# Two transformer blocks on one core: another order of loads, modulation pieces and first norm

## The chip, the cores and the metric

The kernel runs on one core of a Trainium2 chip. The metric is the time on the device of one execution, in microseconds (us). An instruction or a row is located by its line in the kernel file (L2190 is line 2190). The engines are PE (TensorE, matrix products; PEld are its weight loads), DVE (VectorE), ACT (ScalarE), POOL (GpSimd) and SP (SyncE), which here only issues DMAs. Each engine executes its own list of instructions in order, and waits on semaphores for the others.

## The reference

All in float32, for 512 tokens of width 1024, with 256 context tokens. The part that matters here is the first lines of the first block:

```python
sh1, sc1, gt1, sh2, sc2, gt2 = split(silu(c) @ w_mod + b_mod, 6)        # for the tokens
csh1, csc1, ...              = split(silu(c_ctx) @ w_mod + b_mod, 6)    # for the context
pc = (rmsnorm(ctx, norm1_g) * (1 + csc1) + csh1) @ w_in
px = (rmsnorm(x, norm1_g) * (1 + sc1) + sh1) @ w_in
```

`rmsnorm` divides each token by the root of the mean of its squares. From `pc` and `px` come a gated linear attention in both directions and a differential attention; their outputs go through `w_out`, then follow a gated feed-forward layer and a second block (pooling and forgetting attention, attention to a memory of 256 tokens, a convolved feed-forward layer). The scalar `lam` of the differential attention is made of the exponentials of two sums of products (lambda).

## The kernel before

Everything is held transposed: features on the 128 partitions, tokens along the free dimension; `xT` is 8 tiles (k = 0 to 7) of 128 x 512, `cmT` 8 of 128 x 256. A product of float32 quality is made of three passes in the type fp32r: high part of the weights by high part of the data, high by low, and low by high. For each unit of weights (128 x 1024, 512 KB) SP loads `raw` (4 buffers), ACT writes the high part `whi` (`hi`, L560 to 565, 3 buffers), and DVE, or POOL for units 1 and 2, the low part `wlo` (`lo`, L1239 to 1246, and L2008 to 2011). Units 0 to 3 are those of the first projection (`gqk`), two values of k each; unit 4 is that of the next product (`gd`).

There is no planner; the order is written out by hand for each engine, and this is the order at the start.

- SP (from L517): 16 pieces of the modulation weights (`mod1`, 512 KB each, two values of k by 512 columns), the context behind the sixth, the tokens behind the ninth, weight unit 0 behind the thirteenth, then units 1 to 3 and eight constants. Pieces 14 and 15 wait until PE has finished pieces 0 and 1 (`mdp`).
- PE (from L2157): eight transposes turn the condition (both vectors) into columns; ACT puts SiLU on them. The 16 pieces are multiplied in order, each by two columns, in plain float32 (L2190; four matmul records per piece), to rows of 512 results in banks 0, 1, 6 and 7, four pieces each. Ahead of piece 10 stand `turn_mods(0)` (eight small transposes that turn the first half of the rows to columns, L2166), the sum of the context's squares over the partitions (a product with ones, L2173), and the small lambda product in bank 3 (L2182); ahead of piece 11 the sum of the tokens' squares. Behind piece 15 come two products that broadcast the raw condition to all partitions (L2195, banks 0 and 1), and then the first projection (L2232 to 2242): for each k four banks (0 to 3) of 128 x 512 for the tokens, then two (4 and 5) of 128 x 256 for the context, each of three passes. `turn_mods(1)` follows k = 1. `fill(b)` waits for whoever last read bank b; `unit(j)` waits for `lo` of unit j.
- ACT (from L592): the squares of the context's and the tokens' tiles (L613), with the copies `mod_rows(0)` of the first two result rows (L602) between them; the roots (`root`: Ln, Exp, Square); the exponential of the lambda sums (L617, it frees bank 3); then a loop over i = 0 to 15, tile k = i // 2 of the tokens (i even) or of the context (i odd): it writes the high part of the normed tile (L630). At i = 4 stand `mod_rows(1)` and SiLU of the broadcast condition (L624, `cbx`), which frees banks 0 and 1; after i = 1, 3 and 7 `hi` of unit 0, 1 and 2.
- DVE (from L1271): adds the squares (L1277), finishes the roots (`newton`, L1255 and 1257), and in a loop over the same i, at i = 0 and 8, `first_mods` (L1287 and 1290: gains and shifts from the turned rows), `first_norm(i)` (L1300: tile x gain x root), `first_rest(i - 1)` (L1307: low part), and `lo(0)` at i = 2. Units 3 and up are split behind the loop.
- From there on `cbx` serves DVE for dot products that make the other modulations (L1328).

The products of k need their tile's low part (`x_ready`, `xc_ready`).

Of the kernel before, what the change touches and what calls it, by code (L numbers as in the profile page):

```python
# [16 lines left out]
D = 1024  # L17
# [168 lines left out]
def build(nc, ap, out):  # L186
# [6 lines left out]
    with ctx:  # L193
# [314 lines left out]
        def _(e):  # L508
# [8 lines left out]
            for n in range(16):  # L517
                w.wait_ge(s.mdp, n - 13)
                j = NU + n
                src = ap["weights"][offs[j]:offs[j + 1]].rearrange("(p k c) -> p k c", p=128, c=512)  # L520
                e.dma_start(mod1[n][:, :, :], src).then_inc(s_m[n % 14], 16)
                if n == 5:
                    e.dma_start(cmT[:, :, :], ap["ctx"]).then_inc(s.cm, 16)
                if n == 8:
                    e.dma_start(xT[:, :, :], ap["x"]).then_inc(s.x, 16)
                if n == 12:
                    load(0)
            for j in range(1, 4):
                load(j)
# [19 lines left out]
        def _(e):  # L549
# [48 lines left out]
            def mod_rows(half):  # L598
                for j in range(2):
                    w.wait_ge(s.mdp, 8 * half + 4 * j + 4)  # L600
                    b = 6 + j if half else j
                    e.activation(mrow[half][0:2, j, :], bank(b)[0:2, :], ACT.Copy).then_inc(s.mdr, 1)  # L602

            for q in range(16):
                if q == 8:
                    mod_rows(0)
                n, src, first = (256, cmT, acc_c) if q < 8 else (512, xT, acc)
                if q % 8 == 0:
                    w.wait_ge(*((s.cm, 16) if q == 0 else (s.x, 16)))
                elif q >= 4:  # L610
                    w.wait_ge(s.sqs, adds(q - 4))
                dst = tmp[q % 4] if q % 8 else first
                e.activation(dst[:, 0:n], src[:, q % 8, :], ACT.Square).then_inc(s.sq, 1)  # L613
            w.wait_ge(s.g_const, 1)
            root("ctx", bank(4, 256), 256, D)
            w.wait_ge(s.lam_p, 1)
            e.activation(small[:, 4:6], bank(3, 2), ACT.Exp).then_inc(s.lam_a, 1)  # L617
            root("x", bank(5), 512, D)
            for i in range(16):
                if i == 4:  # L620
                    mod_rows(1)
                    for j in range(2):
                        w.wait_ge(s.p_cb, 2 + j)
                        e.activation(cbx[:, 512 * j:512 * j + 512], bank(j), ACT.Silu).then_inc(s.cb, 1)  # L624
                        table[0] = "silu"
                k, ctx_ = i // 2, i % 2
                n = 256 if ctx_ else 512
                dst = (hch if ctx_ else hxh)[:, k, :]
                w.wait_ge(s.mt, nt_at["A", i])
                e.activation(dst, tmp[i % 4][:, 0:n], ACT.Identity, bias=modv[:, k, ctx_:ctx_ + 1]).then_inc(s.mh, 1)  # L630
                if i in (1, 3, 7):
                    hi(i // 3)
# [601 lines left out]
        def _(e):  # L1234
# [43 lines left out]
            newton("ctx", bank(4, 256), 256, D)  # L1278
            newton("x", bank(5), 512, D)

# [22 lines left out]
            def first_rest(i):  # L1303
# [4 lines left out]
                                       f((hch if c else hxh)[:, k, :]), ALU.add, ALU.subtract).then_inc(s.ml, 1)  # L1308

            for i in range(16):  # L1310
                if i % 8 == 0:
                    first_mods(i // 2)
                first_norm(i)
                if i:
                    first_rest(i - 1)
                if i == 2:
                    lo(0)
            first_rest(15)
# [770 lines left out]
        def _(e):  # L2089
# [80 lines left out]
            def first_sums(b, size, value, sum_):  # L2170
                w.wait_ge(s.sqs, value)
                w.wait_ge(s.g_const, 2)
                e.matmul(bank(b, size), ones[:, :], sum_[:, 0:size], start=True, stop=True).then_inc(s.p_sum, 1)  # L2173

            w.wait_ge(s.cb, 1)
            for n in range(16):
                if n == 10:
                    turn_mods(0)
                    first_sums(4, 256, 7, acc_c)
                    w.wait_ge(s.lam_v, 1)  # L2180
                    fill(3)
                    e.matmul(bank(3, 2), ones[:, :], small[:, 2:4], start=True, stop=True).then_inc(s.lam_p, 1)  # L2182
                    freed[3] = [(s.lam_a, 1)]
                if n == 11:
                    first_sums(5, 512, 14, acc)
                b = (0, 1, 6, 7)[n // 4]
                w.wait_ge(s_m[n % 14], 16 * (n // 14 + 1))
                for kk in range(2):
                    k = 2 * (n % 4) + kk
                    mm = e.matmul(bank(b)[0:2, :], cols_c[:, k, :], mod1[n][:, kk, :], start=(k == 0), stop=(k == 7))  # L2190
                mm.then_inc(s.mdp, 1)
            for j in range(2):
                w.wait_ge(s.mdr, j + 1)
                w.wait_ge(s.g_const, 2)
                e.matmul(bank(j), ones[0:1, :], crow[0:1, 512 * j:512 * j + 512], start=True, stop=True).then_inc(s.p_cb, 1)  # L2195
                freed[j] = [(s.cb, 2 + j)]
            freed[2] = [(s.mdv, 2)]
# [27 lines left out]
            for k in range(8):  # L2225
# [17 lines left out]
                if k % 2:  # L2243
                    mm.then_inc(s.used, 1)
                if k == 1:
                    turn_mods(1)
                    freed[6] = [(s.mdv, 4)]
                    freed[7] = [(s.mdr, 4)]
# [684 lines left out]
```

## Time and profile before

| what | value |
|---|---|
| median of 3 runs | 1654.87 us (1654.38 to 1655.11) |
| the profiled execution: its time | 1654.45 us |
| the profiled execution: its span | 1652.8 us |
| PE busy | 1578.4 us (96%) |
| DVE, ACT, POOL busy | 57%, 44%, 8% |
| DMA queue of SP | 152 MB |

The span runs from the first to the last instruction; its own time has 1.65 us more. A busy PE isn't a PE at its peak, since matmuls overlap and their ends are modelled. The page cuts the span into 40 slices of 41.3 us. In a timeline a row has the start and the length in us, engine, line, operation, what is written and read, the shapes and the number of merged instructions, and in brackets how long the engine had been idle and who released it.

### The profile page before, as it was taken

The numbers are of one execution on the slowest core, as the hardware profiler recorded it, in microseconds if no ns is written. First come the engines' busy times: TensorE is split into PE (matmuls) and PEld (weight loads), VectorE is DVE, ScalarE is ACT, GpSimd is POOL, SyncE is SP. The second block draws the span as 40 slices with busy tenths as digits, with TensorE's granted clock in tenths as the row PEclk, the third lists the DMA queues.
The fourth block names the chain that finished last, engine by engine and source line by source line (L and its number), as shares of the span: only waits on it lengthen the run. The fifth ranks groups of instructions, "written<-read, shape, count | busy, mean of one in ns | idle before, by whom it ended". The sixth has DMA issues, their size and how long they took to land.

```text
span 1652.8 us, 19178 instructions
## 1 busy us (share of the span) xinstructions
PE 1578.4 (96%) x7606; PEld 1241.7 (75%) x7606; DVE 938.5 (57%) x1441; ACT 732.8 (44%) x1132; POOL 124.2 (8%) x89
## 2 busy tenths in 40 slices
PE   8999999889899999999999899999977999999999
PEld 2777876677688888888878677788665788888885
DVE  3676777884834433334645555366556686257743
ACT  4444445675433222223443767455455443234432
POOL 0100213530000000000000111130010000000000
PEclk9999999699999999999999999999988999999999
DMA  9441111102433233222232222143202232333221
GB/s 375 156 166 52 52 52 59 56 1 88 155 132 136 75 106 113 99 78 92 90 102 70 75 67 65 63 129 103 77 27 89 65 115 70 109 115 97 79 91 53
DMA packets 47950, 156.60 MB, mean 95 GB/s; under 512 B 5587, under 2 KB 10323, under 8 KB 47350
## 3 DMA queue, kind: packets, MB, share of 16 engines
q1 hardware_dynamic: 47280, 152.00, 27.8%
q10 hardware_dynamic: 582, 3.38, 0.6%
q8 instruction: 61, 1.00, 0.2%
q14 instruction: 27, 0.22, 0.0%
HBM read 153.26 MB, written 2.10 MB: 94 GB/s over the span
## 4 chain that ended last, share of the span: by engine, by line
PE 79%; DVE 11%; ACT 6%; issue 3%; DMA 0%; POOL 0%; ACTq 0%; DVEq 0%
PE pall L2112 19%; PE pall L2113 18%; PE pall L2114 18%; PE pall L2596 2%; PE pall L2130 1%; PE pall L2132 1%; PE pall L2131 1%; PE pall L2148 1%; PE pall L2598 1%; PE pall L2597 1%; PE pall L2150 1%; PE pall L2149 1%; DVE wlo L1244 1%; DVE statd L1589 1%; PE pall L2190 1%
## 5 line engine op out<-in xcount | busy, mean ns | idle before, releaser
L1244 DVE TENSOR_TENSOR wlo<-raw,whi 128x1024 fp32r<-128x1024 f32 (+2 forms) x261 | 290.5, 1114 | 315.3 <-ACT whi L564 315.2
L564 ACT ACTIVATE whi<-raw 128x1024 fp32r<-128x1024 f32 (+2 forms) x263 | 247.0, 941 | 212.6 <-PE pall L2114 177.3
L2112 PE MATMUL pall<-h5h,whi 128*128 128x512 f32 x320 | 125.7, 393 | 2.5 <-DVE wlo L1244 2.5
L2113 PE MATMUL pall<-h5l,whi 128*128 128x512 f32 x320 | 125.2, 391 | 0.0
L2114 PE MATMUL pall<-h5h,wlo 128*128 128x512 f32 x320 | 125.0, 391 | 0.0
L2112 PE MATMUL pall<-h2h,whi 128*128 128x512 f32 x320 | 124.5, 389 | 0.0
L2113 PE MATMUL pall<-h2l,whi 128*128 128x512 f32 x320 | 124.5, 389 | 0.0
L2114 PE MATMUL pall<-h2h,wlo 128*128 128x512 f32 x320 | 124.5, 389 | 0.0
L2112 PEld LDWEIGHTS pall<-h5h,whi 128*128 128x128 f32 x320 | 60.4, 189 | 15.6 <-issue 3.1
L2114 PEld LDWEIGHTS pall<-h5h,wlo 128*128 128x128 f32 x320 | 60.5, 189 | 12.7
L2113 PEld LDWEIGHTS pall<-h5l,whi 128*128 128x128 f32 x320 | 60.5, 189 | 12.7 <-issue 0.2
L2114 PEld LDWEIGHTS pall<-h2h,wlo 128*128 128x128 f32 x320 | 60.1, 188 | 12.6
L2113 PEld LDWEIGHTS pall<-h2l,whi 128*128 128x128 f32 x320 | 60.1, 188 | 12.4
L2112 PEld LDWEIGHTS pall<-h2h,whi 128*128 128x128 f32 x320 | 60.1, 188 | 12.4
L2112 PE MATMUL pall<-fh,whi 128*128 128x512 f32 x176 | 68.5, 389 | 0.0
L2113 PE MATMUL pall<-fl,whi 128*128 128x512 f32 x176 | 68.5, 389 | 0.0
L2114 PE MATMUL pall<-fh,wlo 128*128 128x512 f32 x176 | 68.5, 389 | 0.0
L2112 PE MATMUL pall<-ch,whi 128*128 128x512 f32 x176 | 68.5, 389 | 0.0
L2113 PE MATMUL pall<-cl,whi 128*128 128x512 f32 x176 | 68.5, 389 | 0.0
L2114 PE MATMUL pall<-ch,wlo 128*128 128x512 f32 x176 | 68.5, 389 | 0.0
L946 ACT ACTIVATE fh<-tmp 128x512 fp32r<-128x512 f32 x22 | 13.9, 632 | 95.1 <-DVE tmp L1695 95.1
L1912 DVE TENSOR_TENSOR pall<-pall,R 128x512 f32<-128x512 f32 x48 | 33.1, 694 | 35.2 <-PE pall L2114 31.2
(460 smaller groups left out, 3644.8 us busy)
## 6 DMA issues: line engine op xcount, KB each, us to landing
raw<-in_weights SPq DMA_DIRECT2D x204, 512.0 KB, 3.5
mraw<-in_wmod SPq DMA_DIRECT2D x32, 512.0 KB, 5.1
mod<-in_weights SPq DMA_DIRECT2D x16, 512.0 KB, 12.2
raw<-in_weights SPq DMA_DIRECT2D x25, 256.0 KB, 2.5
raw<-in_weights SPq DMA_DIRECT2D x32, 192.0 KB, 2.3
xT<-in_x SPq DMA_DIRECT2D x1, 2048.0 KB, 17.0
xT<-in_x ACTq DMA_DIRECT2D x1, 2048.0 KB, 8.2
out_y<-xT SPq DMA_DIRECT2D x8, 256.0 KB, 2.1
```

Of the source, the lines that this page charges most:

```text
L564: e.activation(whi[j % 3][:, 0:cols(j)], raw[j % 4][:, 0:cols(j)], ACT.Copy).then_inc(s.hi, 1)
L1244: e.tensor_tensor(wlo[j % 3][:, 0:n], raw[j % 4][:, 0:n], f(whi[j % 3][:, 0:n]), ALU.subtract).then_inc(s.lo_v, 1)
L1589: e.reduce_max(sd[:, col:col + 1], bank(2 * dpair[c, n], 768), AX.X).then_inc(s.mx, 1)
L1912: e.tensor_tensor(bank(b), bank(b), r, ALU.mult).then_inc(s.rq, 1)
L2112: e.matmul(o_, a[:, kk, :], xh(k), start=(k == 0), stop=False)
L2113: e.matmul(o_, a[:, kk, :], xl(k), start=False, stop=False)
L2114: mm = e.matmul(o_, b[:, kk, :], xh(k), start=False, stop=(k == nk - 1))
L2130: e.matmul(bank(o_), a[:, k % 2, c], xh(k), start=(k == 0), stop=False)
L2131: e.matmul(bank(o_), a[:, k % 2, c], xl(k), start=False, stop=False)
L2132: mm = e.matmul(bank(o_), b[:, k % 2, c], xh(k), start=False, stop=(k == 7))
L2148: e.matmul(bank(o_), h_, a[:, kk, :], start=(k + kk == 0), stop=False)
L2596: e.matmul(bank(b), a[:, k, :], xh[:, k, :], start=(k == 0), stop=False)
```

## The change

SP issues the context and the tokens behind the fourth piece, weight unit 0 behind the eighth and unit 1 behind the twelfth. PE broadcasts the condition first (banks 6 and 7), does pieces 0 to 8 with the context's sum behind piece 5, turns the first half, sums the tokens' squares, and does pieces 9 to 11 and the lambda product; pieces 12 to 15 stand inside the projection behind k = 1, and `turn_mods(1)` behind k = 2. ACT does `cbx` first, then all squares, the context's root, `mod_rows(0)`, `hi(0)`, and the tokens' root; lambda's exponential stands at i = 6 of the loop, `mod_rows(1)` at i = 8. DVE does `first_mods(0)` and `lo(0)` before the tokens' root, and `first_rest(7)` before `first_mods(4)`.

```diff
--- before.py
+++ after.py
@@ -519,13 +519,12 @@
                 j = NU + n
                 src = ap["weights"][offs[j]:offs[j + 1]].rearrange("(p k c) -> p k c", p=128, c=512)
                 e.dma_start(mod1[n][:, :, :], src).then_inc(s_m[n % 14], 16)
-                if n == 5:
+                if n == 3:
                     e.dma_start(cmT[:, :, :], ap["ctx"]).then_inc(s.cm, 16)
-                if n == 8:
                     e.dma_start(xT[:, :, :], ap["x"]).then_inc(s.x, 16)
-                if n == 12:
-                    load(0)
-            for j in range(1, 4):
+                if n in (7, 11):
+                    load(n // 4 - 1)
+            for j in range(2, 4):
                 load(j)
             for dst, name in consts:
                 e.dma_start(dst, ap[name]).then_inc(s.const, 16)
@@ -601,9 +600,10 @@
                     b = 6 + j if half else j
                     e.activation(mrow[half][0:2, j, :], bank(b)[0:2, :], ACT.Copy).then_inc(s.mdr, 1)
 
+            for j in range(2):
+                w.wait_ge(s.p_cb, 2 + j)
+                e.activation(cbx[:, 512 * j:512 * j + 512], bank(6 + j), ACT.Silu).then_inc(s.cb, 1)
             for q in range(16):
-                if q == 8:
-                    mod_rows(0)
                 n, src, first = (256, cmT, acc_c) if q < 8 else (512, xT, acc)
                 if q % 8 == 0:
                     w.wait_ge(*((s.cm, 16) if q == 0 else (s.x, 16)))
@@ -613,22 +613,21 @@
                 e.activation(dst[:, 0:n], src[:, q % 8, :], ACT.Square).then_inc(s.sq, 1)
             w.wait_ge(s.g_const, 1)
             root("ctx", bank(4, 256), 256, D)
-            w.wait_ge(s.lam_p, 1)
-            e.activation(small[:, 4:6], bank(3, 2), ACT.Exp).then_inc(s.lam_a, 1)
+            mod_rows(0)
+            hi(0)
             root("x", bank(5), 512, D)
             for i in range(16):
-                if i == 4:
+                if i == 6:
+                    w.wait_ge(s.lam_p, 1)
+                    e.activation(small[:, 4:6], bank(3, 2), ACT.Exp).then_inc(s.lam_a, 1)
+                if i == 8:
                     mod_rows(1)
-                    for j in range(2):
-                        w.wait_ge(s.p_cb, 2 + j)
-                        e.activation(cbx[:, 512 * j:512 * j + 512], bank(j), ACT.Silu).then_inc(s.cb, 1)
-                        table[0] = "silu"
                 k, ctx_ = i // 2, i % 2
                 n = 256 if ctx_ else 512
                 dst = (hch if ctx_ else hxh)[:, k, :]
                 w.wait_ge(s.mt, nt_at["A", i])
                 e.activation(dst, tmp[i % 4][:, 0:n], ACT.Identity, bias=modv[:, k, ctx_:ctx_ + 1]).then_inc(s.mh, 1)
-                if i in (1, 3, 7):
+                if i in (3, 7):
                     hi(i // 3)
 
 
@@ -1276,7 +1275,6 @@
                     w.wait_ge(s.sqs, adds(q) - 1)
                     e.tensor_tensor(sum_[:, 0:n], sum_[:, 0:n], tmp[q % 4][:, 0:n], ALU.add).then_inc(s.sqs, 1)
             newton("ctx", bank(4, 256), 256, D)
-            newton("x", bank(5), 512, D)
 
             def first_mods(k):
 
@@ -1307,14 +1305,16 @@
                 e.scalar_tensor_tensor((hcl if c else hxl)[:, k, :], tmp[i % 4][:, 0:n], modv[:, k, c:c + 1],
                                        f((hch if c else hxh)[:, k, :]), ALU.add, ALU.subtract).then_inc(s.ml, 1)
 
+            first_mods(0)
+            lo(0)
+            newton("x", bank(5), 512, D)
             for i in range(16):
-                if i % 8 == 0:
-                    first_mods(i // 2)
+                if i == 8:
+                    first_rest(7)
+                    first_mods(4)
                 first_norm(i)
-                if i:
+                if i and i != 8:
                     first_rest(i - 1)
-                if i == 2:
-                    lo(0)
             first_rest(15)
             lo(2)
             w.wait_ge(s.cb, 3)
@@ -2172,28 +2172,34 @@
                 w.wait_ge(s.g_const, 2)
                 e.matmul(bank(b, size), ones[:, :], sum_[:, 0:size], start=True, stop=True).then_inc(s.p_sum, 1)
 
+            w.wait_ge(s.g_const, 2)
+            for j in range(2):
+                e.matmul(bank(6 + j), ones[0:1, :], crow[0:1, 512 * j:512 * j + 512], start=True, stop=True).then_inc(s.p_cb, 1)
+                freed[6 + j] = [(s.cb, 2 + j)]
             w.wait_ge(s.cb, 1)
-            for n in range(16):
-                if n == 10:
-                    turn_mods(0)
-                    first_sums(4, 256, 7, acc_c)
-                    w.wait_ge(s.lam_v, 1)
-                    fill(3)
-                    e.matmul(bank(3, 2), ones[:, :], small[:, 2:4], start=True, stop=True).then_inc(s.lam_p, 1)
-                    freed[3] = [(s.lam_a, 1)]
-                if n == 11:
-                    first_sums(5, 512, 14, acc)
+
+            def mod_piece(n):
                 b = (0, 1, 6, 7)[n // 4]
+                if n % 4 == 0:
+                    fill(b)
                 w.wait_ge(s_m[n % 14], 16 * (n // 14 + 1))
                 for kk in range(2):
                     k = 2 * (n % 4) + kk
                     mm = e.matmul(bank(b)[0:2, :], cols_c[:, k, :], mod1[n][:, kk, :], start=(k == 0), stop=(k == 7))
                 mm.then_inc(s.mdp, 1)
-            for j in range(2):
-                w.wait_ge(s.mdr, j + 1)
-                w.wait_ge(s.g_const, 2)
-                e.matmul(bank(j), ones[0:1, :], crow[0:1, 512 * j:512 * j + 512], start=True, stop=True).then_inc(s.p_cb, 1)
-                freed[j] = [(s.cb, 2 + j)]
+
+            for n in range(9):
+                mod_piece(n)
+                if n == 5:
+                    first_sums(4, 256, 7, acc_c)
+            turn_mods(0)
+            first_sums(5, 512, 14, acc)
+            for n in range(9, 12):
+                mod_piece(n)
+            w.wait_ge(s.lam_v, 1)
+            fill(3)
+            e.matmul(bank(3, 2), ones[:, :], small[:, 2:4], start=True, stop=True).then_inc(s.lam_p, 1)
+            freed[3] = [(s.lam_a, 1)]
             freed[2] = [(s.mdv, 2)]
             freed[4] = [(s.rsum, job["ctx"])]
             freed[5] = [(s.rsum, job["x"])]
@@ -2243,6 +2249,9 @@
                 if k % 2:
                     mm.then_inc(s.used, 1)
                 if k == 1:
+                    for n in range(12, 16):
+                        mod_piece(n)
+                if k == 2:
                     turn_mods(1)
                     freed[6] = [(s.mdv, 4)]
                     freed[7] = [(s.mdr, 4)]
```

## Rows read from the trace of the kernel before

**Rows 1.** The page, 40 slices of the span: granted clock of PE, and GB/s

```profile
PEclk9999999699999999999999999999988999999999
...
GB/s 375 156 166 52 52 52 59 56 1 88 155 132 136 75 106 113 99 78 92 90 102 70 75 67 65 63 129 103 77 27 89 65 115 70 109 115 97 79 91 53
```

**Rows 2.** Timeline of all engines, 0 to 110 us: the start

```profile
6.08 1.01 PE L2159 MATMUL pall<-ident,crow 2*128 2x2 f32 x8 [6.08 <-DMA ident<-in_ident]
...
7.37 19.61 PE L2190 MATMUL pall<-mod,small 128*2 128x512 f32 x40 [0.27 <-ACT small L596]
...
10.74 0.13 PEld L2190 LDWEIGHTS pall<-mod,small 128*2 128x2 f32 x1 [0.73 <-issue]
...
11.59 0.13 PEld L2190 LDWEIGHTS pall<-mod,small 128*2 128x2 f32 x1 [0.73 <-issue]
12.23 0.09 PEld L2190 LDWEIGHTS pall<-mod,small 128*2 128x2 f32 x1 [0.51 <-issue]
12.66 0.09 PEld L2190 LDWEIGHTS pall<-mod,small 128*2 128x2 f32 x1 [0.34 <-issue]
...
14.00 0.42 ACT L613 ACTIVATE acc_c<-cmT 128x256 f32<-128x256 f32 x1 [6.68 <-DMA cmT<-in_ctx]
```

**Rows 3.** The same timeline: the sums and the norm

```profile
27.50 0.70 PE L2173 MATMUL pall<-acc_c,ones 128*128 128x256 f32 x2
...
30.76 1.13 PE L2173 MATMUL pall<-acc,ones 128*128 128x512 f32 x2 [0.64 <-DVE acc L1277]
...
35.83 0.75 DVE L1300 SCALAR_TENSOR_TENSOR tmp<-xT,gsv,R 128x512 f32<-128x512 f32 x1
...
37.38 0.75 DVE L1307 SCALAR_TENSOR_TENSOR hxl<-tmp,modv,hxh 128x512 fp32r<-128x512 f32 x1 [0.40 <-ACT hxh L630]
```

**Rows 4.** The same timeline: the broadcasts and the start of the projection

```profile
40.49 1.98 PE L2195 MATMUL pall<-crow,ones 1*128 1x512 f32 x4
...
45.21 0.77 PE L2232 MATMUL pall<-hxh,whi 128*128 128x512 f32 x1 [2.74 <-ACT cbx L624]
```

**Rows 5.** Timelines of PE (50 to 78 us), then DVE, then ACT (45 to 135 us)

```profile
54.33 0.65 PE L2166 MATMUL pall<-ident,mrow 2*128 2x2 f32 x8
...
58.48 0.40 PE L2232 MATMUL pall<-hxh,whi 128*128 128x512 f32 x1
...
75.77 0.39 PE L2112 MATMUL pall<-hxh,whi 128*32 128x512 f32 x1
...
55.01 0.24 DVE L1287 TENSOR_TENSOR modv<-pall,vec 128x8 f32<-128x8 f32 x2 [5.86 <-PE pall L2166]
...
55.55 0.75 DVE L1300 SCALAR_TENSOR_TENSOR tmp<-xT,gsv,R 128x512 f32<-128x512 f32 x1
56.23 0.48 DVE L1307 SCALAR_TENSOR_TENSOR hcl<-tmp,modv,hch 128x256 fp32r<-128x256 f32 x1
...
65.32 1.56 DVE L1244 TENSOR_TENSOR wlo<-raw,whi 128x1024 fp32r<-128x1024 f32 x2 [0.45 <-ACT whi L564]
...
61.55 0.51 ACT L630 ACTIVATE hch<-tmp,modv 128x256 fp32r<-128x256 f32 x1
```

**Rows 6.** Windows: length; busy us of PE, PEld, DVE, ACT, POOL; granted clock; DMA

```profile
42.75:43.00 0.25, 0.00 (x0) 0.00 (x0) 0.25 (x1) 0.25 (x1) 0.25 (x1) 0.50 0.00 0
925.40:928.10 2.70, 0.07 (x2) 0.07 (x1) 2.12 (x7) 2.29 (x5) 0.00 (x0) 1.00 0.06 26
1316.00:1319.30 3.30, 3.30 (x8) 2.53 (x9) 2.46 (x5) 1.35 (x2) 0.00 (x0) 0.50 0.56 159
```

**Rows 7.** Timeline of PE, 284 to 360 us: first passes of query blocks

```profile
316.37 0.76 PE L2448 MATMUL pall<-Kh,Qh 64*128 64x512 f32 x1 [2.39 <-ACT e L866]
...
323.24 0.49 PE L2448 MATMUL pall<-Kh,Qh 64*128 64x512 f32 x1
...
327.25 0.50 PE L2448 MATMUL pall<-Kh,Qh 64*128 64x512 f32 x1
...
346.61 0.47 PE L2448 MATMUL pall<-Kh,Qh 64*128 64x512 f32 x1 [1.97 <-ACT e L866]
```

## The prediction

> **What bounds the kernel now.** I read first the page: the granted clock is full in nearly every slice, and DMA is busy in the first slice, where about 375 GB/s are moved [rows 1]. Then the chain of waits and the timeline of the first 80 us, since the whole change lies there. TensorE (PE) works from 6.08 us, on 64 passes of modulation weights (four per piece, 16 pieces). In them the weight loads of L2190 start 0.85 us apart at first and 0.43 us apart later; one spacing of 0.64, from 11.59 to 12.23, puts the change of clock at 12.0 [rows 2]. Then come the first half of the turned modulations, the two sums, and the norm on VectorE (DVE) [rows 3]. The first projection starts only at 45.21: PE has to finish all 16 pieces and two broadcasts of the condition, and waits 2.74 us for ScalarE (ACT), which turns the broadcast into `cbx` in banks 0 and 1 [rows 4]. The second turned half follows at 54.33, in the middle of the projection; from there PE runs without a pause to 75.77, where the next product begins [rows 5]. Behind it PE runs on for a long stretch, and its later short waits are for ACT and DVE work that hangs on PE's own results. So what counts is how early PE reaches the point that is now at 75.77.
>
> **The change, part by part.** The kernel gets the same work in another order; I follow PE, because it is late at each step.
>
> *Broadcasts first.* They begin where the eight transposes of the condition end, 6.08 + 1.01 = 7.1 [rows 2]. Four passes at the slow spacing of 0.85 take 3.4 us (1.98 at full clock [rows 4]), so pieces start at 10.5. They use banks 6 and 7, and ACT has long emptied these when piece 8 comes. When the clock rises then, the trace of before doesn't show. From below: as before, at 12.0. From above: the rise counts from the first piece, as it came 4.7 us after 7.37 before [rows 2]; that is 15.2. I take 15.2, because after the same one-row broadcasts at 40.49 the clock had fallen by 42.75, when PE had rested for only 0.3 us [rows 4, 6]; a wait of 1.97 us at 346.61 leaves it full [rows 1, 7]. The difference costs 1.6 us.
>
> *Pieces and sums.* By 15.2 there are (15.2 - 10.5)/0.85 = 5.5 passes done; the other 18.5 of pieces 0 to 5 take 7.9 us at 0.427: 23.1. The context's sum has 0.70 [rows 3], of which the next matmul covers the end; I take 0.5: 23.6. Pieces 6 to 8, 12 passes, 5.1: 28.8. The turned half 0.6 (0.65 with its tail [rows 5]): 29.4. Loads: before, six pieces and the context, 4.2 MB, had landed when ACT began its squares at 14.00 [rows 2]; now pieces 0 to 3, both inputs and piece 4 are 5.8 MB, so piece 4 lands at about 14.0 + 1.6/0.375 = 18.2 at the page's rate [rows 1]. PE asks for it at 15.2 + 10.5 x 0.43 = 19.7. The cover is 1.5 us, and later pieces gain (1.4 us to land, 1.7 to multiply). Were it gone, PE would start that much later and no more. x's squares and sum on DVE end near 23.5 and are hidden behind piece 8; so DVE no longer decides when the sum at 30.76 [rows 3] starts.
>
> *Norm.* From the start of the sum over x to the first norm it is 35.83 - 30.76 = 5.07, of which 0.54 are the modulations (55.01 to 55.55 for the other half), now done ahead [rows 3, 5]: 4.5. The first norm starts at 33.9 instead of 35.83, and its low part is ready 2.3 later (37.38 + 0.75 against 35.83): 36.2. `hi(0)` and `lo(0)` lie ahead of it, in idle time. PE meanwhile does the sum (1.06, to the first pass after it), pieces 9 to 11 (5.1) and the lambda product (0.3, between nothing and the 0.7 of the context's): 35.9. So the projection starts at 36.2, nine us earlier than now.
>
> *What is late next: bank 3.* The lambda product sits in bank 3, and the exponential that frees it is moved on ACT from before the loop to its seventh turn. PE can do banks 0 to 2 only, nine passes of 0.23 = 2.1: 38.3. In the second half of the loop the sixth high part ends 61.55 + 0.51 - 55.55 = 6.5 after the first norm [rows 5]; with `hi(1)` between I take 6.6, so the bank is free at 33.9 + 6.6 = 40.5. PE waits 2.2 us. Behind that wait the rest of k = 0 (1.4) and k = 1 (3.46, by 75.77 - 58.48 = five such steps [rows 5]) end at 45.4.
>
> *Last four pieces, inside.* 16 passes, 6.8: 52.2. They landed long before. k = 2: 55.7, turned half: 56.3. Before it ended at 54.33 + 0.6 = 54.9, so this is 1.4 later.
>
> *The end of the projection.* PE has k = 3, 4, 5 left before the fourth unit of weights: 56.3 + 10.4 = 66.7. But the low half of that unit comes after DVE's whole loop: before, it started at 65.32 and took 1.1 (two of them end at 66.9) [rows 5]. It moves by the 1.4, less the 0.4 of `first_rest(7)`, which now precedes the modulations (56.23 to the next norm) [rows 5]: 67.4. PE waits 0.7, and k = 6, 7 end at 74.3. Against 75.77 that is 1.5 earlier; small steps between kinds of work, each 0.1 and not in my sum, take 0.3 of it. **Result: -1.2 us.**
>
> *Edits with one answer.* The saved switches of ACT's table and the earlier weights 0 and 1 on SP lie beside work of PE; SP's fixed waits for pieces 14 and 15 (`mdp` 1 and 2) end by about 15.6, while the queue has MBs ahead of them. The dots with `cbx` come after weights that ACT makes; nothing waits for them there. The gates after the projection follow PE's results and move with it.
>
> The profiled execution took 1654.45 for a span of 1652.8; the median of the runs is 1654.87, 0.4 more. So the profile after should have a span near 1651.6 and the median should be 1653.7.
>
> **The rule that is weighed.** The rows above put the rise of the clock at one place of one execution [rows 2]. The Trainium skill (TensorE: Matmul & The Clock Gate, Part 1: The HAM clock gate) says that the point of the rise doesn't restart with a kernel and varies between runs of the same one. By it my 1.6 us would be anything from 0 to 1.6, and the forecast -1.2 to -2.8. The three runs of before lie within 0.73 us, so such a spread isn't seen here; I keep -1.2, and the early rise is a rival.
>
> **The rivals.**
> 1. *The clock rises at 12.0 as before* (broadcasts count as work). Everything up to the turned half comes 1.6 earlier: -2.8. For it: nothing but PE being busy. Against it: rows 6 after the broadcasts. 0.13.
> 2. *The clock falls in the new 2.2 us wait.* For it: from 1316.0 to 1319.3 the clock is at half, behind a wait of PE; against it, PE stood nearly still for 2.7 us at 925.4 and kept it [rows 6]. Price: 3.4 us at half are 1.7 us of PE: +0.5 with the late rise, -1.1 with the early one. 0.17.
> 3. *A slow stretch of the clock goes away.* In the slice of 289 to 331 us the clock is 0.6 [rows 1], in the diff attention; there a query block takes 323.24 - 316.37 = 6.9 us, and at full clock 4.0 [rows 7]. It began after a short gap of PE, and may not when the work arrives 1 us earlier. Over three or four blocks that is worth up to 4 x 2.9 = 11.6 as an upper bound, and half of it, 6, as ACT's own waits stay: 1648. 0.17.
> 4. *The other side: such a stretch is added.* Place: the wait of 1.97 us at 346.61 for ACT's `e` [rows 7], at the end of which the clock was full before. If the clock falls there and stays down, each block costs 2.9; from two blocks on (5.8 - 1.2 = +4.6) the kernel is slower by over 0.2%: 1659.5. Against it: the same wait held before. 0.08.
> 5. *The change does nothing*: the order of the projection is bound by the second turned half, which is late in both. Then 1654.9. This is what is left if the wait at the fourth unit is 1.2 longer. 0.1.
>
> **How the numbers follow.** My forecast gets 0.35, at 1653.7. A measurement can tell about 0.2%, 3.3 us, from no change. Forecast and rivals 1, 2 and 5 lie all within it, 0.75 together, but their terms carry errors of 1 us or so, and rival 1 with the sum 1 us better is at the edge: I move 0.09 to faster and 0.01 to slower. Faster: 0.17 + 0.09 = 0.26. Slower: 0.08 + 0.01 = 0.09. Within: 0.65. The likeliest case's own range is 1652.2 to 1655.6 (rise of the clock, with or without the fall). For 8 in 10 I reach into rival 3 down to 1649.0, and up to 1656.3.
>
> **What would show it.** Right: the profile has L2195 first at 7.1 with 0.85 per pass, the projection at 36 to 37, a wait of PE for ACT's `small` of about 2 us after nine passes, pieces again at 45 to 52, the turned half near 56, a short wait for `wlo`, and the next product at 74.5. Wrong: full clock at 12; pieces waiting for DMA at 18; a half clock at 39 to 43; the next product at 74.5 but a total off by over 2 us, which would put the reason into the later stretches of the clock.

## The result and the profile after

The changed kernel takes 1659.86 us (median of 7 runs, 1658.89 to 1661.02); the kernel before, beside it, 1654.87 (7 runs, 1653.80 to 1655.73). The ratio is 1.0032, with a 95% interval of 1.0021 to 1.0044: 5.0 us slower, where 1.2 faster was forecast. The profiled execution has 1659.81 us and a span of 1658.2.

The order of the work is as forecast up to 38.5 us, and then not. These are rows of the timeline of the changed kernel, one for each step (start and length in us, engine, line, operation, operands, and in brackets the idle time and who ended it); lines differ a little from those of before.

```profile
7.00 3.76 PE L2177 MATMUL pall<-crow,ones 1*128 1x512 f32 x4
10.69 12.09 PE L2188 MATMUL pall<-mod,small 128*2 128x512 f32 x24
...
36.34 0.47 PE L2238 MATMUL pall<-hxh,whi 128*128 128x512 f32 x1 [0.51 <-DVE hxl L1305]
...
38.10 1.04 ACT L563 ACTIVATE whi<-raw 128x1024 fp32r<-128x1024 f32 x1
...
39.23 2.44 POOL L2011 TENSOR_TENSOR wlo<-raw,whi 128x1024 fp32r<-128x1024 f32 x1 [38.28 <-ACT whi L563]
...
39.38 2.57 DVE L1298 SCALAR_TENSOR_TENSOR tmp<-cmT,gsv,R 128x256 f32<-128x256 f32 x1
...
41.98 0.51 ACT L629 ACTIVATE hch<-tmp,modv 128x256 fp32r<-128x256 f32 x1 [2.16 <-DVE tmp L1298]
42.40 0.15 ACT L622 ACTIVATE small<-pall 128x2 f32<-128x2 f32 x1
...
42.60 0.80 PE L2238 MATMUL pall<-hxh,whi 128*128 128x512 f32 x1 [3.94 <-ACT small L622]
```

The broadcasts take their slow 3.76 us, and the projection starts at 36.34, against 45.21 before [rows 4] and 36.2 in the forecast. Then PE stops for 3.94 us, where 2.2 were forecast, for the exponential in bank 3 (L622). What delays it is DVE: its sixth norm lasts 2.57 us instead of 0.48, and it lies in the time in which POOL makes the low part of weight unit 1. Here are three windows of the changed kernel (length; busy us of PE, PEld, DVE, ACT, POOL; granted clock; DMA).

```profile
38.50:41.30 2.80, 0.16 (x1) 0.00 (x0) 2.80 (x3) 1.32 (x2) 2.07 (x1) 1.00 0.92 314
42.60:48.20 5.60, 5.60 (x16) 4.72 (x17) 2.61 (x6) 2.65 (x4) 2.57 (x2) 0.51 0.28 97
...
396.30:399.50 3.20, 3.20 (x8) 2.21 (x8) 2.13 (x3) 0.93 (x2) 0.00 (x0) 0.50 0.00 0
```

In the wait the clock is still full; from 42.6 to 48.2 it is at half (0.51), and PE does what is left of k = 0 and k = 1 in 7.6 us instead of the 4.9 of the forecast. The kernel before has such a stretch too, at the start of its projection:

```profile
45.20:49.60 4.40, 4.39 (x11) 3.46 (x12) 2.96 (x5) 3.24 (x6) 0.00 (x0) 0.51 0.34 123
```

So the change does away with one stretch of half clock, in which PE worked for about 4.3 us, and brings another, of about 5.5 us of work. Later landmarks on PE in the changed kernel:

```profile
50.19 7.03 PE L2188 MATMUL pall<-mod,small 128*2 128x512 f32 x16
...
60.80 0.65 PE L2166 MATMUL pall<-ident,mrow 2*128 2x2 f32 x8
...
73.08 0.50 PE L2238 MATMUL pall<-hxh,whi 128*128 128x512 f32 x1 [1.05 <-DVE wlo L1243]
...
80.12 0.39 PE L2112 MATMUL pall<-hxh,whi 128*32 128x512 f32 x1
```

These answer to rows 5: the last four pieces start at 50.19; the second turned half is at 60.80 (54.33 before, 55.7 forecast); the wait for the fourth unit's low part ends at 73.08 (67.4 forecast); the next product is at 80.12 (75.77 before, 74.3 forecast). The lag of 4.35 us behind the kernel before stays the same up to about 320 us: nothing between the projection and that point makes it up or adds to it. From there the two profiles differ in where the clock falls. In the changed kernel it is at half from 351.9 to 358.7 and, at the end of another pair of one-row broadcasts, from 396.3 to 399.5; in the kernel before it is at half from 370.4 to 373.8, and full at those two places. By the times of the changed kernel, the lag goes to 5.1 us at 364, to 3.7 at 377 and to 5.5 at 400, and at the end of the span it is 5.4: 1.1 more than at the next product.

### The profile page after: what moved, and what is told of

It is laid out like the page before. It is cut to its first block, busy times and chain, and to the rows that moved or that the text cites. A ratio compares the mean times of both kernels' runs of the same rounds, so it can differ in the third digit from the quotient of the medians.

```text
span 1658.2 us, 19178 instructions
## 1 busy us (share of the span) xinstructions
PE 1582.9 (95%) x7606; PEld 1245.1 (75%) x7606; DVE 938.3 (57%) x1441; ACT 730.5 (44%) x1130; POOL 125.1 (8%) x89
## 4 chain that ended last, share of the span: by engine, by line
PE 79%; DVE 11%; ACT 6%; issue 3%; DMA 0%; POOL 0%; ACTq 0%; DVEq 0%
PE pall L2112 19%; PE pall L2113 18%; PE pall L2114 18%; PE pall L2605 2%; PE pall L2188 1%; PE pall L2130 1%; PE pall L2132 1%; PE pall L2131 1%; PE pall L2148 1%; PE pall L2607 1%; PE pall L2606 1%; PE pall L2149 1%; PE pall L2150 1%; DVE wlo L1243 1%; ACT whi L563 1%
## 5 line engine op out<-in xcount | busy, mean ns | idle before, releaser
L2112 PEld LDWEIGHTS pall<-h5h,whi 128*128 128x128 f32 x320 | 60.4, 189 | 15.7 <-issue 3.1
## 6 DMA issues: line engine op xcount, KB each, us to landing
mod<-in_weights SPq DMA_DIRECT2D x16, 512.0 KB, 15.2
```

The source lines that it names most:

```text
L2112: e.matmul(o_, a[:, kk, :], xh(k), start=(k == 0), stop=False)
```

## The experiments

Each was timed beside the kernel before on the same chip; there were three chips. The kernel before has 1655.80 us beside experiments 1 to 4 (35 runs), 1655.80 beside 5 to 8 (29 runs) and 1656.27 beside 9 and 10 (21 runs). Each ratio is to that one, so between chips ratios are compared and not times. Times there spread wider than in the first comparison (1653.6 to 1658.8 for the kernel before), so each verdict rests on the time and on the landmarks of its profile, which is one execution. "Next product" is the first matmul of the product behind the projection: 75.77 before, 80.12 after.

**1. Lambda's exponential at i = 2.**

```diff
-                if i == 6:
+                if i == 2:
                     w.wait_ge(s.lam_p, 1)
                     e.activation(small[:, 4:6], bank(3, 2), ACT.Exp)
```

> The changed kernel with one edit: lambda's exponential, which frees bank 3, stands at i = 2 of ACT's loop instead of i = 6. Theory A (the loss is the wait for bank 3, 3.94 us in the changed kernel, and the half clock that it leaves behind, 5.7 us from 42.6 to 48.3, worth 2.85): no wait of PE inside k = 0, full clock to the second turned half, which comes near 54.0 instead of 60.80, next product (L2112) near 73.3 instead of 80.12, time near 1653. Rival B (the loss is at the start, in the broadcasts and pieces at the low clock, and the wait only takes slack that would be waited elsewhere): the next product stays at 78 or later, time 1657 or more.

Measured: 1653.77 us, ratio 0.9985 (0.9976 to 0.9993). Rows of its timeline:

```profile
36.86 0.17 ACT L622 ACTIVATE small<-pall 128x2 f32<-128x2 f32 x1
...
37.32 0.47 PE L2238 MATMUL pall<-hxh,whi 128*128 128x512 f32 x1 [0.50 <-DVE hxl L1305]
...
40.36 2.62 DVE L1298 SCALAR_TENSOR_TENSOR tmp<-cmT,gsv,R 128x256 f32<-128x256 f32 x1
...
55.04 0.65 PE L2166 MATMUL pall<-ident,mrow 2*128 2x2 f32 x8
...
74.33 0.39 PE L2112 MATMUL pall<-hxh,whi 128*32 128x512 f32 x1
```

PE doesn't wait inside k = 0, the clock is full up to the second turned half at 55.04, and the next product is at 74.33, 5.8 earlier, though this execution started its projection 1.0 later. DVE's norm is stretched here too (2.62 us at 40.36); nobody on PE's way waits for it. One number in the order of ACT's loop turns the change from slower into slightly faster than before. Rival B falls.

**2. The high part of unit 1 at i = 7**, and so POOL's low part later.

```diff
-                if i in (3, 7):
-                    hi(i // 3)
+                if i == 7:
+                    hi(2)
```

> The changed kernel with one edit: the high part of weight unit 1 (and so POOL's low part of it) is made at i = 7 instead of i = 3; lambda's exponential stays at i = 6. Theory A2 (DVE's sixth norm took 2.57 us instead of 0.48 because POOL's low part of unit 1 ran beside it, 39.23 to 41.67): that norm takes 0.48, the exponential comes near 39.4, PE waits about 1 us for bank 3 and the clock stays full; next product near 74.5, time near 1654. Rival (the length of that norm has another cause, or the order on ACT alone sets the wait): the norm stays at 2.5 us, PE's wait at 3 us or more, time near 1659.

Measured: 1658.08 us, ratio 1.0011 (1.0002 to 1.0019). Rows of its timeline, and the window behind PE's wait:

```profile
34.89 0.75 DVE L1298 SCALAR_TENSOR_TENSOR tmp<-xT,gsv,R 128x512 f32<-128x512 f32 x1
...
40.37 0.48 DVE L1298 SCALAR_TENSOR_TENSOR tmp<-cmT,gsv,R 128x256 f32<-128x256 f32 x1
...
41.29 0.15 ACT L622 ACTIVATE small<-pall 128x2 f32<-128x2 f32 x1
...
41.50 0.50 PE L2238 MATMUL pall<-hxh,whi 128*128 128x512 f32 x1 [1.88 <-ACT small L622]
...
76.47 0.39 PE L2112 MATMUL pall<-hxh,whi 128*32 128x512 f32 x1
```

```profile
41.50:46.00 4.50, 4.50 (x24) 3.88 (x25) 2.69 (x6) 3.61 (x5) 1.37 (x1) 1.00 0.01 4
```

The norm takes 0.48 us, the wait falls from 3.94 to 1.88, the clock stays full in this execution, and the next product is at 76.47: the mechanism is as expected. The edit also takes 1.0 us of ACT's work (the high part) from ahead of the exponential, but in the changed kernel ACT idled 2.16 us for the norm behind that work, so the wait didn't hang on it. The wait is longer than the 1 us that I gave it. That this execution ran 1.0 late from the start doesn't explain it, since the projection is late by the same 1.0 (37.33); my expectation had the exponential 5.5 us behind the first norm (39.4 against 33.9), and it comes 6.4 behind it (34.89 to 41.29). Bank 3 starts 6.6 behind the first norm, which is the figure of the prediction. Less the 1.0, the next product would be near 75.5, hardly ahead of the 75.77 of the kernel before: by this estimate the change would have been worth next to nothing even without the stretched norm and the fallen clock. The time is 4 us over the expectation. The profiled execution is one of three at 1655.1 to 1655.4 us (mean clock 0.981); the other eight lie at 1658.0 to 1659.4 (0.976 to 0.980). A fall of the clock in the remaining wait would explain them, and was not seen in a profile; falls elsewhere later on (experiment 9) could do the same, so this stays open.

**3. The kernel before with the broadcasts first**, and with them, on ACT, `cbx` (it leaves i = 4 of the loop); nothing else moved. The comments are added here, and some lines on banks are left out.

```diff
+            for j in range(2):          # ACT, ahead of the squares
+                w.wait_ge(s.p_cb, 2 + j)
+                e.activation(cbx[:, 512 * j:512 * j + 512], bank(6 + j), ACT.Silu).then_inc(s.cb, 1)
...
+            for j in range(2):          # PE, ahead of piece 0
+                e.matmul(bank(6 + j), ones[0:1, :], crow[0:1, 512 * j:512 * j + 512], ...)
+                freed[6 + j] = [(s.cb, 2 + j)]
...
-            for j in range(2):          # PE, behind piece 15
-                e.matmul(bank(j), ones[0:1, :], crow[0:1, 512 * j:512 * j + 512], ...)
```

> The kernel before with only the condition's broadcasts moved to the start (banks 6 and 7, cbx ahead of the squares); loads, pieces and the rest as before. Theory A: the start loses 3.3 us (four passes at 0.85), the end of the pieces gains the 2.0 of the broadcasts, the wait of 2.74 and the half clock behind it (about 2.1), so the projection starts near 43 and the next product is near 71.5 instead of 75.77: time near 1651. Rival B (broadcasts at the low clock are what costs): next product at 76 or later, time 1655 or more.

Measured: 1653.28 us, ratio 0.9986 (0.9974 to 0.9997). Rows of its timeline:

```profile
43.00 0.50 PE L2234 MATMUL pall<-hxh,whi 128*128 128x512 f32 x1
...
44.80 2.80 POOL L2010 TENSOR_TENSOR wlo<-raw,whi 128x1024 fp32r<-128x1024 f32 x1 [43.85 <-ACT whi L564]
44.86 0.48 DVE L1299 SCALAR_TENSOR_TENSOR tmp<-cmT,gsv,R 128x256 f32<-128x256 f32 x1
...
46.31 1.84 DVE L1306 SCALAR_TENSOR_TENSOR hxl<-tmp,modv,hxh 128x512 fp32r<-128x512 f32 x1 [0.97 <-ACT hxh L629]
...
72.02 0.39 PE L2111 MATMUL pall<-hxh,whi 128*32 128x512 f32 x1
```

The projection starts at 43.00 without a wait and at full clock, and the next product is at 72.02. This one part of the change, alone, gives more at this landmark (3.75 us) than all of it was forecast to give. The time is 2.3 over the 1651 expected and below the 1655 of rival B, and falls by 2.5 us against the kernel before, less than the landmark says. The norm beside POOL's low part of unit 1 takes only 0.48 here; in its place POOL's row has 2.80 us, and DVE's next operation beside it is the one that is stretched (1.84 instead of 0.75).

**4. The exponential at i = 2, and the broadcasts behind piece 3.**

```diff
                 mod_piece(n)
+                if n == 3:
+                    w.wait_ge(s.g_const, 2)
+                    for j in range(2):
+                        e.matmul(bank(6 + j), ones[0:1, :], crow[0:1, 512 * j:512 * j + 512], ...)
...
```

> As the kernel with the exponential at i = 2, and the two broadcasts behind piece 3 instead of first. Theory A3 (one-row broadcasts at the start delay the rise of the clock, 15.4 against 12.0, and run at 0.85 per pass themselves): pieces start at 7.3, full clock from 12.0, turned half of the modulations 1.7 us earlier than with broadcasts first, time 1.7 us less. Rival (the rise doesn't depend on what runs): no difference at the turned half but the 0, time the same within 0.5.

Measured: 1655.25 us, ratio 0.9995 (0.9986 to 1.0003). Rows of PE's timeline:

```profile
16.59 1.98 PE L2192 MATMUL pall<-crow,ones 1*128 1x512 f32 x4
...
23.50 0.70 PE L2173 MATMUL pall<-acc_c,ones 128*128 128x256 f32 x2 [1.41 <-DVE acc_c L1276]
...
30.19 0.66 PE L2166 MATMUL pall<-ident,mrow 2*128 2x2 f32 x8 [0.75 <-ACT mrow L601]
```

The broadcasts take 1.98 us at full clock, and the clock rose at 12.2 as in the kernel before, so the first half of the theory holds (its 15.4 for the changed kernel was misread: the clock rises at 14.0 there). But the gain is given back in two waits that weren't there: 1.41 us for the context's sum and 0.75 for the copied rows, because ACT puts `cbx` ahead of its squares and so starts them at 19.1 instead of 11.5. The next product is at 74.94, 0.6 behind experiment 1, and the time 1.5 above it, where I expected 1.7 less: a miss of mine.

**5. The changed kernel with the last four pieces ahead of the projection.**

```diff
             freed[3] = [(s.lam_a, 1)]
+            for n in range(12, 16):
+                mod_piece(n)
...
-                if k == 1:
-                    for n in range(12, 16):
-                        mod_piece(n)
```

> The changed kernel with the last four pieces ahead of the projection again (behind the lambda product); lambda's exponential stays at i = 6. Theory A: with 6.9 us of pieces between the lambda product and the projection, bank 3 is free (42.6 to 43.6) before PE asks for it at 45; no wait, full clock. The projection starts near 43, the second turned half near 53.5, PE waits about 1.3 for the fourth unit's low part, next product near 72.7, against 80.12 in the changed kernel: time near 1652.5. Rival (what costs is the order of loads or the start): next product at 77 or later.

Measured: 1654.12 us, ratio 0.9989 (0.9979 to 0.9999). Rows of PE's timeline:

```profile
53.69 0.65 PE L2166 MATMUL pall<-ident,mrow 2*128 2x2 f32 x8
...
73.01 0.39 PE L2112 MATMUL pall<-hxh,whi 128*32 128x512 f32 x1
```

Next product at 73.01 (72.7 expected), with the exponential still at i = 6 and the norm still stretched (2.57 us at 39.75); the time is 1.6 over the 1652.5 expected. So the wait for bank 3 needs two of the change's moves together: the exponential moved back, and the pieces, which would have covered it, moved behind.

**6. The kernel before with the broadcasts behind piece 3.** The edit is that of experiment 3, with the two matmuls ahead of piece 4 instead of piece 0.

> The kernel before with only the condition's broadcasts moved, to behind piece 3. Theory A3: pieces start at 7.3 and the clock rises near 12 as in the kernel before, broadcasts take 2.0 us at full clock, ACT's squares of the context come at 18 and delay nothing, so the next product is near 70.2, 1.8 earlier than with broadcasts first (72.02): time near 1650. Rival (as behind the exponential's move, the gain is lost to a wait for the context's or tokens' sum on ACT and DVE): next product at 71.5 to 72, time within 0.5 of the kernel with broadcasts first.

Measured: 1652.54 us, ratio 0.9982 (0.9974 to 0.9991), the lowest of all, though its interval overlaps those of experiments 1, 3, 5 and 7. Rows of PE's timeline:

```profile
7.45 8.31 PE L2196 MATMUL pall<-mod,small 128*2 128x512 f32 x16 [0.27 <-ACT small L596]
15.70 1.98 PE L2179 MATMUL pall<-crow,ones 1*128 1x512 f32 x4
...
70.66 0.39 PE L2111 MATMUL pall<-hxh,whi 128*32 128x512 f32 x1
```

Next product at 70.66, 5.1 earlier than in the kernel before (70.2 expected); the time falls by 3.3, to 2.5 over the 1650 expected. The clock rose at 10.1 here, 1.9 before that of the kernel before; by the spacings of 0.85 and 0.43 us that is worth about 1 of the 5.1 us (an estimate), and it is chance. Here the squares of the tokens stand behind `mod_rows(0)` anyway, so ACT's later start delays nothing.

**7. The exponential at i = 2, and weight unit 3 split early**, while both engines wait for PE.

```diff
                 if i == 8:
+                    hi(3)
                     mod_rows(1)
...
                     first_rest(7)
+                    lo(3)
                     first_mods(4)
```

> The kernel with the exponential at i = 2, and the fourth weight unit split (high part on ACT ahead of mod_rows(1), low part on DVE ahead of the second modulations), in time in which both engines wait for PE. Theory: the wait of PE for wlo at k = 6 (1.04 us) goes; the next product comes 1.0 earlier than 74.33, time 1 us less than with the exponential alone. Rival (the split delays the second modulations or the norms behind them): the wait moves to the norms of k = 4, no gain.

Measured: 1653.48 us, ratio 0.9986 (0.9977 to 0.9994). Rows of its timeline:

```profile
46.93 2.34 POOL L2013 TENSOR_TENSOR wlo<-raw,whi 128x1024 fp32r<-128x1024 f32 x1 [3.96 <-ACT whi L563]
...
47.83 2.52 DVE L1244 TENSOR_TENSOR wlo<-raw,whi 128x1024 fp32r<-128x1024 f32 x1 [1.32 <-ACT whi L563]
...
73.30 0.39 PE L2114 MATMUL pall<-hxh,whi 128*32 128x512 f32 x1
```

The next product is at 73.30, 1.0 earlier, and PE has no wait at k = 6; the median moves by 0.3 only, which these runs can't tell from 0 or 1. DVE's low part again takes 2.52 us where it meets POOL's, here in time that nobody needs.

**8. The changed kernel again**, no edit.

> The changed kernel as it is, on the chip of these experiments. Theory A: PE waits 3.9 us for bank 3 again and the clock falls in every run, so it stays about 4 to 5 us over the kernel before on the same chip. Rival (the low clock behind the wait is chance): its times fall into two groups 3 us apart, as those of the kernel with the later unit 1 did (1655.2 and 1658 to 1659).

Measured: 1661.02 us (5 runs, 1659.49 to 1661.89), ratio 1.0031 (1.0019 to 1.0043). PE waits 3.93 us and the next product is at 79.80. Its clock fell too (0.54 from 42.6 to 48.2). None of the five lies 3 us below the rest, and none of the seven of the first comparison: the rival falls, as far as 12 executions tell.

**9. PE kept busy in the wait**, by 16 matmuls whose results nobody reads.

```diff
+                    if k == 0 and i == 3:
+                        fill(7)
+                        for _ in range(16):
+                            e.matmul(bank(7), a[:, 0, c], hxh[:, 0, :], start=True, stop=True)
```

> The changed kernel with 16 matmuls of 128 x 512 into bank 7, whose results nobody reads, between banks 2 and 3 of k = 0: PE works where it had waited, and bank 3 still comes when ACT frees it. Theory A (two costs: the wait itself, 3.9 us, and the half clock behind it, 5.7 us long, worth 2.9): bank 3 starts at 42.4 to 43 as in the changed kernel, all of it at full clock, the second turned half comes near 58.0 instead of 60.80, next product near 77.2 instead of 80.12, time near 1657.5. Rival (the half clock costs nothing, because DVE or ACT would be waited for anyway): turned half and next product as in the changed kernel within 0.5.

Measured: 1659.02 us (1656.40 to 1661.39), ratio 1.0018 (1.0009 to 1.0027). Rows of PE's timeline, and the window behind the wait:

```profile
39.32 3.79 PE L2239 MATMUL pall<-hxh,whi 128*128 128x512 f32 x16
43.51 0.50 PE L2242 MATMUL pall<-hxh,whi 128*128 128x512 f32 x1 [0.41 <-ACT small L622]
...
59.23 0.65 PE L2166 MATMUL pall<-ident,mrow 2*128 2x2 f32 x8
...
78.53 0.39 PE L2112 MATMUL pall<-hxh,whi 128*32 128x512 f32 x1
```

```profile
43.51:48.50 4.99, 4.99 (x27) 4.31 (x27) 2.61 (x6) 2.67 (x4) 1.96 (x1) 1.00 0.31 105
```

Bank 3 starts at 43.51, later than in the changed kernel, as the projection of this execution starts 0.9 late (37.19); from there to the turned half it takes 59.23 - 43.51 = 15.7 us instead of 60.80 - 42.60 = 18.2. The half clock behind the wait is worth 2.5 us, and the rival falls. (58.0 and 77.2 were expected for the turned half and the next product; both come 1.2 to 1.3 later, 0.9 of it from the late start.) The ratio is 1.0018 against 1.0031 in experiment 8, some 2 us less, with intervals that overlap; six of 11 runs are at 1656.4 to 1659.0, five at 1660.6 to 1661.4, and the profiled one is of the latter: it is 1.6 ahead of the changed kernel at the next product and 1.1 behind at 811 us, after clock falls at 272 and 364 us that the profile of the changed kernel doesn't have. So where the clock falls later on differs between these two profiles, at a price of 2.7 us.

**10. The kernel before with the high part of unit 1 at i = 7.**

```diff
-                if i in (1, 3, 7):
+                if i in (1, 7):
```

> The kernel before with the high part of unit 1 at i = 7 instead of i = 3. Theory A2: in the kernel before, too, POOL's low part of unit 1 (42.29 to 44.63) stretched a norm on DVE (2.56 us at 42.36), beside PE's work, at no cost; with the edit that norm takes 0.48, and the projection starts up to 1.0 earlier, only because the 0.95 of the high part no longer stands ahead of cbx on ACT: next product 74.8 to 75.8, time the same to 1 less. Rival (the stretched norm cost the kernel before something as well): 2 us or more less.

Measured: 1656.47 us, ratio 1.0007 (0.9998 to 1.0016). First the kernel before, POOL and DVE, then this one, DVE and PE:

```profile
42.29 2.34 POOL L2011 TENSOR_TENSOR wlo<-raw,whi 128x1024 fp32r<-128x1024 f32 x1 [41.34 <-ACT whi L564]
...
42.36 2.56 DVE L1300 SCALAR_TENSOR_TENSOR tmp<-cmT,gsv,R 128x256 f32<-128x256 f32 x1
```

```profile
42.29 0.48 DVE L1300 SCALAR_TENSOR_TENSOR tmp<-cmT,gsv,R 128x256 f32<-128x256 f32 x1
...
44.20 0.77 PE L2232 MATMUL pall<-hxh,whi 128*128 128x512 f32 x1 [1.81 <-ACT cbx L624]
...
75.17 0.39 PE L2112 MATMUL pall<-hxh,whi 128*32 128x512 f32 x1
```

```profile
44.20:49.40 5.20, 5.20 (x12) 4.11 (x13) 2.96 (x5) 4.04 (x7) 0.43 (x1) 0.50 0.01 3
```

The same stretched norm stood in the kernel before, at 42.36, beside PE's wait for `cbx`, and cost nothing that shows: with 0.48 instead, the projection starts 1.0 earlier, because the high part of unit 1 no longer stands ahead of `cbx` on ACT, the next product comes 0.6 earlier, and the time doesn't change. The window is the start of its projection: behind a wait of 1.81 us the clock is at half.

## Why the prediction was wrong

The step that failed is the wait for bank 3: forecast at 2.2 us with full clock behind it, it was 3.94 us, because POOL's work stretched a norm that the forecast took at its usual length, and behind it PE did some 5.5 us of its work at half clock. The parts follow in the prediction's order.

*The broadcasts first, the pieces, the sums, the norm, the start of the projection:* right. 3.76 us for the broadcasts (3.4), projection at 36.34 (36.2), lines in the order given; piece 4 never waited for DMA. That the first norm came at 33.91, as forecast to the digit, is partly luck: the sum over x started 0.25 early (29.15, not 29.4), and from there to the norm it took 4.76 and not 4.5. The rise of the clock came at 14.0 in this execution, where I took 15.2, by these weight loads of the changed kernel, whose spacing goes from 0.83 to 0.43 us; in experiment 1 it came at 15.9:

```profile
13.20 0.13 PEld L2188 LDWEIGHTS pall<-mod,small 128*2 128x2 f32 x1 [0.72 <-issue]
14.03 0.09 PEld L2188 LDWEIGHTS pall<-mod,small 128*2 128x2 f32 x1 [0.69 <-issue]
14.46 0.09 PEld L2188 LDWEIGHTS pall<-mod,small 128*2 128x2 f32 x1 [0.34 <-issue]
```

The eight profiles with broadcasts first put it between 13.6 and 16.4, so the place of the rise isn't fixed; the two of the changed kernel itself have 14.0 and 13.6. With it the starts of the projection in the changed order spread from 36.1 to 37.6. Of the two ends of the term, 12.0 for a start with broadcasts was never seen; with pieces first it was 12.2 in experiment 4 and 10.1 in experiment 6. The Trainium skill's rule (TensorE: Matmul & The Clock Gate, Part 1: The HAM clock gate), that the place varies between runs of one kernel, agrees with these traces better than my reading of three close times did.

*"What is late next: bank 3":* right in its place, wrong in its size, and this is the step. I had PE wait 2.2 us, with bank 3 free at the first norm plus 6.6, taken from the second half of the loop; it waited 3.94. That half has no POOL in it. In the first half POOL's low part of unit 1 runs from 39.23 to 41.67 and DVE's norm from 39.38 to 41.95; the exponential comes 8.5 us after the first norm and PE goes on 8.7 after it, 2.1 later than forecast. With the norm at its 0.48 us (experiment 2) bank 3 starts 6.6 after the first norm: the term was right but for the stretch. The row that would have told it was in the trace of before (42.36, experiment 10), and I took my durations from its neighbours. The Trainium skill states the rule (SBUF — State Buffer, Who interferes with whom): an instruction of DVE that reads two operands from SBUF contends with one of GpSimd that reads SBUF, and whoever issues first keeps the port. The trace agrees in three places: DVE ends 0.28 us behind POOL here, and 0.29 before; in experiment 7 a low part that met POOL ended 1.08 behind it. In experiments 3 and 6 the two rows start within 0.06 us of each other, the norm keeps its 0.48 and POOL's row is 0.3 to 0.5 us longer instead (2.80), as if DVE had been first there; rows so close can't show the order.

*Rival 2, the clock falls in the wait:* this happened, in both profiles of the changed kernel, and I had given it 0.17 and 1.7 us. It took 2.5 (experiment 9), since PE worked for about 5.5 us at half clock, and not for 3.4. With the wait at 3.9 us it fell in both; at 1.88 us (experiment 2) it stayed full in the profile. That suggests that the longer wait brought the clock with it, but the length alone doesn't decide: in the kernel before and in experiment 10 the clock fell 0.3 us into waits of 2.74 and 1.81 us, right behind one-row broadcasts.

*The end of the projection:* the wait for unit 3 was 1.05 us by the timeline, against 0.7, and it can be removed (experiment 7); with small steps this part took 0.7 more than the sum has. The pieces inside and k = 2 took 10.6 instead of 10.3.

*The sum:* the next product came 5.8 later than the sum has it (74.3): 2.1 from the stretched norm, 2.7 from the slow rest of k = 0 and k = 1, 0.3 and 0.7 from the other steps. With the forecast 1.5 that makes +4.35 against before. The last 1.1 of the profile comes with the places between 324 and 400 us at which the clock falls, and nothing here shows that the change moved them: the profiles of experiments 1, 3, 4, 6, 8 and 9 have a low clock near the one-row broadcasts at 394.6 too, and those of experiments 2, 5, 7 and 10 don't, as that of before doesn't.

*Rivals 3 and 4:* a low clock of 27.3 us (23.9 in experiment 5) that begins between 290 and 301 us is there in all the profiles, so it neither went away nor doubled; the 5.4 us of the span are the start's, and the falls between 324 and 400. *The range:* it ended at 1656.3, and the time is 1659.86. I had the forecast and three of the rivals within 0.2%. That left out the only case that came, because I priced the wait and the clock as separate small terms and let neither grow.

## What to carry to other kernels

When a step is moved, its duration has to be read at the place to which it goes: which other engine works there, and does it read the same memory? A wait of PE on the path can cost more than its length, as the slow time behind it comes on top, 3.9 + 2.5 us here, and a small instruction that frees a PSUM bank belongs ahead of the loop whose tiles it doesn't need. Look for the part of a change that gives most by itself: the broadcasts alone, moved behind piece 3, gave a lower time than both kernels (ratio 0.9982).

## What the runs showed of the hardware that was not expected

- A norm of 128 x 256 on DVE takes 0.48 us alone and 2.56 to 2.62 when it starts 0.07 to 0.16 us behind POOL's subtraction of 2.34 to 2.49 us; a low part of 128 x 1024 takes 2.52 instead of 1.22. Where the norm starts 0.05 or 0.06 us behind (experiments 3 and 6), it is POOL that takes longer, 2.80 us.
- The granted clock reads 1.00 for the first 12 us of the kernel before, while passes start 0.85 us apart there and 0.43 later. In the first microseconds of this profile the spacing tells the clock, and the column does not.
- Behind one-row broadcasts on PE the clock can fall at once: in the kernel before it fell 0.3 us behind the pair at 40.49, in the changed one at 396.3, in the last of the pair at 394.62. It need not: it stayed full behind the pair at 390.66 in the kernel before and behind that in the middle of the pieces in experiments 4 and 6.
